# Attention steps that take two heads at once, with the scores at the end of the step

## What is computed

```python
def attend(q, k, v, bias, valid):
    s = jnp.einsum('bihd,bjhd->bhij', q, k) * (q.shape[-1] ** -0.5)
    s = s + bias[None]
    if valid is not None:
        s = jnp.where(valid, s, -1e30)
    p = jax.nn.softmax(s, axis=-1)
    return jnp.einsum('bhij,bjhd->bihd', p, v)
```

## Time and profile before

| | us |
|---|---|
| median of 3 runs (2169.85 to 2173.09) | 2171.38 |
| the profiled execution | 2167.85 |
| its span from the first to the last instruction | 2166.0 |
| PE busy | 2106.1 (97%) |
| DVE busy | 1409.6 (65%) |
| ACT busy | 957.7 (44%) |
| POOL busy | 275.5 (13%) |
| PE's share of the chain of waits that ended last | 88% |

### The profile page before, as it was taken

The page is one execution under the profiler, slowest core; times in us unless marked ns, Lnnn a source line. Parts: engine busy times, 40 slices in busy tenths (PEclk is TensorE's granted clock), DMA queues, the critical chain, the costliest instruction groups (busy, mean ns, idle before and its releaser), DMA issues.

```text
span 2166.0 us, 38995 instructions
## 1 busy us (share of the span) xinstructions
PE 2106.1 (97%) x16332; PEld 2024.8 (93%) x16332; DVE 1409.6 (65%) x1983; ACT 957.7 (44%) x1494; POOL 275.5 (13%) x250
## 2 busy tenths in 40 slices
PE   6999999999999999999999999999999999999996
PEld 5999999998779899999989999999887889999996
DVE  6767587554447867758886775863544488676674
ACT  6545254232453545435463543532334446363451
POOL 1101002201113100100310000040020040000004
PEclk9999999999999999999999999999999999999998
DMA  6656463222113555645454654522231145464532
GB/s 179 170 144 173 127 167 93 86 79 103 51 51 117 137 157 157 174 118 161 113 136 127 167 155 122 132 88 91 69 114 51 54 128 145 131 167 137 146 108 71
DMA packets 99455, 265.12 MB, mean 122 GB/s; under 512 B 16336, under 2 KB 16384, under 8 KB 99280
## 3 DMA queue, kind: packets, MB, share of 16 engines
q1 hardware_dynamic: 75152, 200.65, 28.4%
q0 software_dynamic: 24128, 61.97, 14.7%
HBM read 255.28 MB, written 11.44 MB: 123 GB/s over the span
## 4 chain that ended last, share of the span: by engine, by line
PE 88%; DVE 7%; ACT 2%; DMA 1%; issue 1%; SPq 0%; DVEq 0%; ACTq 0%
PE pu L688 24%; PE pu L766 21%; PE px L766 21%; PE px L688 12%; PE px L936 2%; PE px L905 2%; DVE wl L1384 1%; PE px L916 1%; DVE zl L1457 1%; PE px L881 1%; PE px L887 1%; DMA raw<-in_w_out 1%; PE pu L715 1%; DVE zf L1438 0%; DVE zxl L1452 0%
## 5 line engine op out<-in xcount | busy, mean ns | idle before, releaser
L1031 ACT ACTIVATE wh<-raw 128x1024 fp32r<-128x1024 f32 (+1 forms) x116 | 118.0, 1017 | 343.7 <-PE pu L688 226.1
L688 PE MATMUL pu<-zh,wh 128*128 128x272 f32 x1056 | 234.2, 303 | 4.7 <-DVE wl L1384 3.7
L580 POOL DMA_DIRECT2D raw_y<-in_gate_up x88 | 77.0, 875 | 1195.3 <-DMA raw_y<-in_gate_up 1195.3
L688 PE MATMUL pu<-zh,wl 128*128 128x272 f32 x1056 | 218.3, 288 | 0.0
L688 PE MATMUL pu<-zl,wh 128*128 128x272 f32 x1056 | 217.9, 288 | 0.0
L1384 DVE TENSOR_TENSOR wl<-raw,wh 128x1024 fp32r<-128x1024 f32 (+2 forms) x140 | 171.6, 1226 | 44.7 <-ACT wh L1031 34.8
L688 PEld LDWEIGHTS pu<-zh,wh 128*128 128x128 f32 x1056 | 164.3, 189 | 12.6 <-DVE wl L1384 4.6
L688 PEld LDWEIGHTS pu<-zl,wh 128*128 128x128 f32 x1056 | 165.9, 188 | 0.0
L688 PEld LDWEIGHTS pu<-zh,wl 128*128 128x128 f32 x1056 | 165.1, 189 | 0.0
L1401 DVE TENSOR_TENSOR wl<-raw,wh 128x1024 fp32r<-128x1024 f32 x88 | 109.5, 1244 | 57.6 <-ACT wh L1054 57.3
L1054 ACT ACTIVATE wh<-raw 128x1024 fp32r<-128x1024 f32 x88 | 93.2, 1059 | 111.2 <-PE px L766 38.6
(11 more groups left out here) (279 smaller groups left out, 6676.8 us busy)
## 6 DMA issues: line engine op xcount, KB each, us to landing
raw<-in_gate_up SPq DMA_DIRECT2D x88, 512.0 KB, 4.0
raw_y<-in_gate_up SPq DMA_DIRECT2D x88, 512.0 KB, 3.9
raw_y<-in_gate_up POOLq DMA_DIRECT2D x88, 512.0 KB, 5.6
raw<-in_down SPq DMA_DIRECT2D x64, 512.0 KB, 3.6
raw<-in_w_in SPq DMA_DIRECT2D x50, 512.0 KB, 3.5
raw_q<-in_gate_up SPq DMA_DIRECT2D x88, 256.0 KB, 3.9
raw<-in_down SPq DMA_DIRECT2D x32, 384.0 KB, 3.9
raw<-in_w_out SPq DMA_DIRECT2D x16, 512.0 KB, 3.5
```

What stands on the lines that cost most here:

```text
L580: pool.dma_start(raw_y[b % 2][:, :, :], gate_up[layer, i, mat, 1].rearrange("p (t c) -> p t c", t=2), accum_op=ALU.add).then_inc(y_summed[ ...
L688: mm = pe.matmul(out[:, a, 0:HALF], w[slot][:, k * P:(k + 1) * P], z[:, k, a * HALF:(a + 1) * HALF], start=(first and n == 0), stop=(last ...
L1031: act.activation(unit_hi[slot][0:rows, 0:columns], raw_of(("unit", U))[0:rows, 0:columns], ACT.Copy)\
```

## The change

The 42 item steps become 22 pair steps (`("PAIR", m)`), spread over the same 56 slots: pair m is items 2m and 2m + 1, the same query tile of both heads. In step m PE now does the value products of pair m - 2 (both heads into one bank, side by side, signalled once), then the transposes of both items of pair m - 1, then the scores of both items of pair m. ACT and DVE follow: ACT copies out both value products, then both transposes, then does both exponentials; DVE does the two reciprocals of pair m - 1, the two sums of squares of pair m - 3, then bias and maximum of both items of pair m. `sc` gets four places; `pt` keeps two. A step has five uses of the ring of four banks where it had three. The norms of the other group's output (`a_norm`) and of the finished pairs of heads (`pair_norm`) move to the steps that answer to the old ones, and one more sum of squares lies behind the last step.

```diff
-    spread([("ITEM", n) for n in range(len(ITEMS) + 2)], 8 * KT + 2, 16 * KT - 6)
+    spread([("PAIR", m) for m in range(PAIRS + 2)], 8 * KT + 2, 16 * KT - 6)
...
-        sc = sb("sc", [P, 2, BAND])
+        sc = sb("sc", [P, 4, BAND])
...
-                uses += [("SC", n)] * (n < len(ITEMS)) + [("PV", n - 2)] * (n >= 2) + [("PT", n - 1)] * (1 <= n <= len(ITEMS))
+            elif kind == "PAIR":
+                uses += [("PV", n - 2)] * (n >= 2) + [("PT", 2 * n - 2), ("PT", 2 * n - 1)] * (1 <= n <= PAIRS)
+                uses += [("SC", 2 * n), ("SC", 2 * n + 1)] * (n < PAIRS)
...
+                    out = use(layer, ("PV", m))
+                    for par in range(2):
+                        h = ITEMS[2 * m + par][1]
+                        wait_for(pe, act_free, layer, ("PT", 2 * m + par))
...
+                            mm = pe.matmul(out[0:rows, par * HD:(par + 1) * HD], pt[0:nk, par, kt * P:kt * P + rows], v,
+                                           start=(kt == 0), stop=(kt == len(vs) - 1))
+                    mm.then_inc(*pe_out.of(("PV", m)))
...
-                        if n < len(ITEMS):
-                            item_scores(n)
                         if n >= 2:
-                            item_values(n - 2)
-                        if 1 <= n <= len(ITEMS):
-                            item_transposes(n - 1)
+                            pair_values(n - 2)
+                        if 1 <= n <= PAIRS:
+                            item_transposes(2 * n - 2)
+                            item_transposes(2 * n - 1)
+                        if n < PAIRS:
+                            item_scores(2 * n)
+                            item_scores(2 * n + 1)
...
-                        wait_for(act, pe_out, layer, ("PV", n - 2))
+                        wait_for(act, pe_out, layer, ("PV", n // 2 - 1))
...
+                    wait_for(act, pe_out, layer, ("PV", m))
+                    for par in range(2):
+                        qt, h = ITEMS[2 * m + par]
+                        rows = TT[qt][1]
+                        wait_for(act, rinv_made, layer, (qt, h))
+                        copy = act.activation(oB[0:rows, qt, h * HD:(h + 1) * HD],
+                                              bank(use_no[("PV", m)])[0:rows, par * HD:(par + 1) * HD], ACT.Copy,
+                                              scale=rinv[0:rows, qt, h:h + 1])
+                    copy.then_inc(*act_free.of(("PV", m)))
...
+                    elif kind == "PAIR":
+                        if n >= 2:
+                            pair_out(n - 2)
+                        if 1 <= n <= PAIRS:
+                            item_probs(2 * n - 2)
+                            item_probs(2 * n - 1)
+                        if n < PAIRS:
+                            item_exp(2 * n)
+                            item_exp(2 * n + 1)
...
+                    elif kind == "PAIR":
+                        if 1 <= n <= PAIRS:
+                            item_inverse(2 * n - 2)
+                            item_inverse(2 * n - 1)
+                        if n >= 3:
+                            item_sum(2 * n - 6)
+                            item_sum(2 * n - 5)
+                        if n < PAIRS:
+                            item_bias(2 * n)
+                            item_bias(2 * n + 1)
...
+                item_sum(len(ITEMS) - 2)
                 item_sum(len(ITEMS) - 1)
```

More of the change, by code:

```diff
@@ L75 @@
 PAIR_ITEMS = 2 * NTT
+PAIRS = len(ITEMS) // 2
 def schedule():
@@ L915, in item_transposes, with pair_values @@
                     for kt, (c0, nk) in enumerate(tiles):
-                        mm = pe.transpose(out[0:nk, kt * P:kt * P + rows], sc[0:rows, n % 2, c0:c0 + nk],
+                        mm = pe.transpose(out[0:nk, kt * P:kt * P + rows], sc[0:rows, n % 4, c0:c0 + nk],
                                           ident[0:rows, 0:rows])
                     mm.then_inc(*pe_out.of(("PT", n)))
-                def item_values(n):
-                    qt, h = ITEMS[n]
+                def pair_values(m):
+                    qt = ITEMS[2 * m][0]
@@ L923, in item_values @@
                     rows = TT[qt][1]
-                    if n == 0:
+                    if m == 0:
                         wait_for(pe, act_free, layer, ("V", NTT - 1))
                         pe.wait_ge(cv_loaded, 16 * layer + 16)
[L928 to L938, removed]
+                    out = use(layer, ("PV", m))
+                    for par in range(2):
+                        h = ITEMS[2 * m + par][1]
+                        wait_for(pe, act_free, layer, ("PT", 2 * m + par))
+                        if qt < NTT - 1:
+                            vs = [(P, bv[0:P, kt, h * HD:(h + 1) * HD]) for kt in range(qt + 1)]
+                        else:
+                            vs = [(P, cv[0:P, kt, h * HD:(h + 1) * HD]) for kt in range(2)]
+                            vs += [(DEC, bv[0:DEC, NTT - 1, h * HD:(h + 1) * HD])]
+                        for kt, (nk, v) in enumerate(vs):
+                            mm = pe.matmul(out[0:rows, par * HD:(par + 1) * HD], pt[0:nk, par, kt * P:kt * P + rows], v,
+                                           start=(kt == 0), stop=(kt == len(vs) - 1))
@@ L1264, in item_exp @@
                     wait_for(act, dve_free, layer, ("SC", n))
-                    act.activation(sc[0:rows, n % 2, 0:nk], sc[0:rows, n % 2, 0:nk], ACT.Exp, scale=-1.0,
+                    act.activation(sc[0:rows, n % 4, 0:nk], sc[0:rows, n % 4, 0:nk], ACT.Exp, scale=-1.0,
                                    bias=nmax[0:rows, qt, h:h + 1],
@@ L1285, in item_probs, with pair_out @@
                             .then_inc(*act_free.of(("PT", n)))
[L1287 to L1291, removed]
+                def pair_out(m):
+                    if m == 0:
                         wait_for(act, pool_ready, layer, "zero_oB")
[L1293 to L1296, removed]
+                    wait_for(act, pe_out, layer, ("PV", m))
[7 more added lines that the diff above has]
+                    copy.then_inc(*act_free.of(("PV", m)))
                 def step(kind, n):
@@ L1314, in step @@
                             .then_inc(*act_free.of(("V", n)))
-                    elif kind == "ITEM":
+                    elif kind == "PAIR":
                         if n >= 2:
[L1317 to L1321, removed]
+                            pair_out(n - 2)
[5 more added lines that the diff above has]
+                            item_exp(2 * n + 1)
                 for b in range(2, len(SIDE_UNITS)):
@@ L1697, in item_bias @@
                     wait_for(dve, pe_out, layer, ("SC", n))
-                    if n >= 2:
-                        wait_for(dve, pe_out, layer, ("PT", n - 2))
-                    dve.tensor_tensor_reduce(out=sc[0:rows, n % 2, 0:nk], in0=bank(use_no[("SC", n)])[0:rows, 0:nk],
+                    if n >= 4:
+                        wait_for(dve, pe_out, layer, ("PT", n - 4))
+                    dve.tensor_tensor_reduce(out=sc[0:rows, n % 4, 0:nk], in0=bank(use_no[("SC", n)])[0:rows, 0:nk],
                                              in1=bt[0:rows, h, at:at + nk], scale=-HD ** -0.5, scalar=3e38,
@@ L1726, in item_sum @@
                     rows = TT[qt][1]
-                    wait_for(dve, act_free, layer, ("PV", n))
+                    wait_for(dve, act_free, layer, ("PV", n // 2))
                     head_sum(("B", qt, h), oB[0:rows, qt, h * HD:(h + 1) * HD],
@@ L1759, in step @@
                             head_sum(("A", n, h), oA[0:rows, n, h * A_DV:(h + 1) * A_DV], ssq[0:rows, n, h:h + 1])
[L1760 to L1764, removed]
-                        if n >= 3:
[L1766 to L1771, removed]
+                    elif kind == "PAIR":
+                        if 1 <= n <= PAIRS:
+                            item_inverse(2 * n - 2)
+                            item_inverse(2 * n - 1)
+                        if n >= 3:
+                            item_sum(2 * n - 6)
[3 more added lines that the diff above has]
+                            item_bias(2 * n + 1)
+                        if 3 <= n < 3 + NTT:
+                            a_norm(n - 3)
+                        if n > NTT and n < PAIRS and n % NTT == NTT - 1:
+                            pair_norm(n // NTT - 1)
                 where = {"v": (vT, 0), "q": (bqT, 0), "k": (bkT, CACHE), "r": (arT, 0)}
```

1 line of the change is left out of this document (removed).

## The result

The changed kernel takes 2141.9 us (median of 4 runs, 2141.07 to 2142.6) against 2170.95 in the same runs for the kernel before: 29.05 us less, a ratio of 0.9865 with a 95% interval of 0.9848 to 0.9882. The prediction was 2148.6 us, 22.8 less, in a range of 2134 to 2164: right in direction, cause and range, and a fifth too small in the gain.

A forecast was written before the change was run, and what follows sets the result against it. PE's own instructions were taken to bound the softmax attention stretch. A layer wins 14.2 + 2.0 + 0.5 - 5.3 = 11.4 us, two layers 22.8, giving a forecast of 2148.6 us in a range of 2134 to 2164.

The forecast's parts named there:

- The bound: Softmax attention stretch: bound by PE's own instructions, busy 111.3 of 112 us, with only 0.5 us of waits.
- Part 1: Scores on PE: two heads' products overlap on the array's halves, saving 14.2 us a layer, bounds 0 and 14.2.
- old waits: PE's two listed waits in the stretch before the change: 0.5 us a layer, expected to go.
- the rival of half an overlap: Second head's scores start only with the first's second record: 8.2 us a layer won, 2155 us; chance 0.15.
- The rival of no overlap: The two heads' scores stay apart: 4.5 us won in all, 2166.9 us; chance 0.10.
- Part 3: Second head's scores on PE wait for ACT to copy both value products out of their bank: 5.3 us a layer lost.
- the rival without a bank wait: ACT copies in time everywhere: 16.7 us a layer won, 2138 us; chance 0.12.
- Part 2: PE's changes between kinds of products: fewer with pairs, saving 2.0 us a layer, bounds 0 and 4.
- The unit's end at slot 96: ACT's 1.05 us weights part stands ahead of the copies for tile 0, which come some 0.5 us late.
- The sum: Gain a layer: 14.2 + 2.0 + 0.5 - 5.3 = 11.4 us; two layers 22.8.
- Cover: Exponentials needed by a step's transposes are ready in time, costed at nothing; up to 2.4 us a step if lost.
- The slower rival: Copies freeing the bank come a whole ACT instruction later every step: with 1.05 us each, 2186 us; chance 0.08.

The follow-up runs named there:

- e3: The changed kernel with the pair's scores at the start of the step and DVE's bias moved to match: 2144.88 us, ratio 0.9877.
- e5: e2 with one more edit on DVE, both heads' biases in the even step and four places in `sc`: 2148.58 us, ratio 0.9905.
- e1: The changed kernel with the second item's transposes put between the two heads' scores on PE, so the scores stand apart: 2168.92 us, ratio 0.9988.
- e6: The changed kernel with one more, unused copy on ACT ahead of the two that free the bank: 2140.72 us in one execution.
- e2: The kernel before with PE's order alone edited, both heads' scores together at even steps, all else one item at a time: 2191.59 us, ratio 1.0088.
- e4: The changed kernel with the step turned round to transposes, scores, value products, and four places in `pt`: 2136.43 us, ratio 0.9843.

## Why the prediction was right, and where its sizes were off

**The bound.** Right: the stretch was PE's own work, and what shortened that work shortened the kernel.

**Part 1, scores side by side, 14.2 us a layer.** Right. Where no bank wait disturbs them (e3, e5) the scores of a layer take 14.3 us; before they took 29.3, in which some 0.8 were old waits. The step from 128 columns to 512, taken on trust, held: 1.07 us for two heads. With it the rival of half an overlap falls, which would have given 1.6 us. The Trainium skill's page "TensorE: Matmul & The Clock Gate", Part 3 (Packing small matmuls), states strict program order for the starts of matmuls; for products on different halves of the array the rows here show otherwise (the last section), and they decide. The rival of no overlap is what e1 builds: 2168.92, where I had put it at 2166.9.

**Part 3, the new wait, 5.3 us a layer.** The mechanism is right (e6) and the size was too large: scores cost 17.55 in the changed kernel and 14.32 without the wait, so 3.2. The waits by tile are 0.29 (tile 0, predicted 0.52), 0.24 (tile 1, 0.39), 0.01 (tile 2, 0.17), none, and 0.26 (sample tile, 0.31). Two latencies of the sum were too long. The first copy starts 0.20 us behind the transposes, not 0.26, and the wake of PE is shorter. ACT's copies for the step above, and the scores of the step at 567 us by how many had begun in three stretches:

```profile
570.17 0.52 ACT L1302 ACTIVATE oB<-px,rinv 128x64 f32<-128x64 f32 x2 [0.82 <-PE px L940]
...
567.00:567.33 0.33, 0.28 (x1) 1.00 0.00 0
567.00:567.36 0.36, 0.31 (x2) 1.00 0.00 0
567.00:567.40 0.40, 0.35 (x3) 1.00 0.00 0
```

In that second step the copies end at 567.29 (0.50 us from 566.79) and the second head begins at 567.34, 0.05 later; I had taken 0.15 from the earlier trace rows, where a copy of transposes wakes value products; in e5 that took 0.14 again (553.72 to 553.86). Why the two differ is not shown. By the number alone the rival without a bank wait, 2138, lies nearer to the 2141.9 measured than the forecast; the rows and e6 decide against it, and the time came so low because Part 2 was too small as well. The unit's end at slot 96 came as worked out, 0.85 us late against 0.9, and it stands alone in the weight loads' list of waits, with the whole pair's scores one after the other:

```profile
PEld px L907 <- ACT oB L1302: 0.6, 1, 0.6
...
593.24 0.61 PE L918 MATMUL px<-ident,sc 128*128 128x128 f32 x4
593.78 1.76 PE L907 MATMUL px<-bkT,bqT 64*128 64x384 f32 x4
595.47 0.40 PE L690 MATMUL pu<-zh,wh 128*128 128x272 f32 x1
```

**Part 2, fewer changes of kind, 2.0 us a layer.** Too small: of the 15.2 won, the scores are 11.7 (29.27 to 17.55), so the rest brought 3.4. The value products gave 2.3 of it (24.2 to 21.9), about the 2.4 that 0.06 for each of 40 items makes, though by two errors that cancel: the change from scores was priced somewhat high, and behind the unit's products value products are faster than their usual pace, four in 0.39 us (569.58 to 569.97) where that pace gives 0.44. The remaining 1.1 lies in the unit's products and transposes together (the table has 1.9, of which some 0.8 are six products fewer ahead of the last value product). There the prices of the prediction make a loss of 0.2: 0.10 for each of 40 items before, 0.21 for each of 20 pairs after. So the difference lies there, and which of their neighbours it belongs to I can't assign.

**The sum.** 14.2 + 2.0 + 0.5 - 5.3 = 11.4 became 14.2 + 3.4 + 0.8 - 3.2 = 15.2. Here 0.8 are the old waits, which cost somewhat more in the distance of scores to value products than the 0.5 of their list. All three errors went the same way; the latencies and the prices of changes had come out of rows with other neighbours.

**Cover.** The exponentials stayed covered: no wait on them stands in PE's list after. The slower rival, an ACT instruction in front of every copy, did not come; e6 shows the price of a short one, 0.11 us for a copy 0.13 later. That slower was possible by another mechanism, e2 shows: a bias that DVE does one step late.

## What to carry to other kernels

Here a second product that used the other half of TensorE's rows cost next to nothing (1.07 us for two heads, 1.05 for one) when it stood right behind the first, in another bank; look for a pair of such products that lies apart in the program and price the whole shorter block. When the order of uses in a ring of banks changes, go through every use and ask what the one it waits for now needs, and which engine's long instruction can stand in front of that: two of the six variants here (e2 and e3) lost by that, and one of them became slower than the start.

## What was not expected of the hardware

The second head's first record starts before the first head's second record, so the two halves do not keep the program's order between them: in the scores of 128 columns of the linear attention and in every undisturbed pair after. That the program has both records of the first head ahead of the second head's shows at 593.78 us, where only the second head waits: two weight loads come at once, two after the copies.

```profile
593.77 0.29 PEld L907 LDWEIGHTS px<-bkT,bqT 64*128 64x128 f32 x2 [0.17 <-issue]
...
594.63 0.29 PEld L907 LDWEIGHTS px<-bkT,bqT 64*128 64x128 f32 x2 [0.56 <-ACT oB L1302]
```

In the step at 567 us the second head, 0.29 us late, still begins before the first head's second record: two records have begun by 567.36 us, the third only by 567.40. A head's second record starts 0.32 us behind its first when 256 keys run alone, so the third is the first head's second.

In e2 six waits of PE of 1.4 to 2.1 us, one at each unit's end, went with a granted clock of 0.89 over the stretch. Falls to the 1.2 GHz level (0.50) lie at 570.2, 587.3, 604.3, 628.2 and 645.3 us, near five of them; the first, up to 551.0, has none (1.00 from 540 to 560). But e1 has such a fall too, at 593.9 us, with no wait in PE's list. In the profile of after the clock fell for short times in the linear attention ahead of the stretch, where the program is that of the kernel before: 0.96 in the mean from 440 to 480 us and 0.97 from 480 to 536, where the kernel before had 1.00; in the profiles of e3 and e4 it did not. Why is not shown.
